# Attention values computed with channels on the partitions and the softmax normalised on GpSimd before the transposes, in a two-block kernel that TensorE fills

## The reference, cut to what matters

```
k_lat, v_lat = mla_kv(z_ckv, z_kr, g_kvnorm[l], w_ukv[l], cos, sin)
k_ctx, v_ctx = mla_kv(zc_ckv, zc_kr, g_kvnorm[l], w_ukv[l], None, None)
q_lat = mla_q(z_cq, g_qnorm[l], w_uq[l], cos, sin)
attn = attend_blocked(q_lat, concatenate([k_ctx, k_lat]), concatenate([v_ctx, v_lat]))
...
s = einsum('bqhd,bkhd->bhqk', q, k) * ATTN_SCALE      # 8 heads, 96 channels
p = softmax(s, axis=-1)
o = einsum('bhqk,bkhd->bqhd', p, v)                   # 64 value channels a head
y = merge_branches(u, conv_module(...), attn @ w_o_mla[l], fourier_mix(...), ...)
if not last:                                          # only in layer 0
    attn_c = attend_dense(q_ctx, k_ctx, v_ctx)        # 256 context queries, 256 keys
```

## Time and profile before

| what | value |
|---|---|
| median of three runs | 2736.62 us (2735.38 to 2741.98) |
| the profiled execution | 2741.98 us |
| span of its instructions | 2740.2 us |
| PE busy | 2623.9 us, 96% of the span |
| DVE, ACT and POOL busy | 62%, 39% and 3% |
| granted TensorE clock, mean | 0.98 |
| attention of layer 0 (first scores to last transposes) | about 1173 to 1294 us |
| attention of layer 1 | about 2355 to 2427 us |

### The profile page before, as it was taken

The page is one execution under the profiler, slowest core; times in us unless marked ns, Lnnn a source line. Parts: engine busy times, 40 slices in busy tenths (PEclk is TensorE's granted clock), DMA queues, the critical chain, the costliest instruction groups (busy, mean ns, idle before and its releaser), DMA issues.

```text
span 2740.2 us, 38792 instructions
## 1 busy us (share of the span) xinstructions
PE 2623.9 (96%) x15874; PEld 2318.9 (85%) x15874; DVE 1711.4 (62%) x2717; ACT 1077.4 (39%) x1652; POOL 69.7 (3%) x64
## 2 busy tenths in 40 slices
PE   7998879799999999999999999999999999998998
PEld 7997669699988888777888888889888888888998
DVE  5766575577777666466654676756555446776664
ACT  5445532445522223334243422323322225555543
POOL 0001013000000000000010000000000000000000
PEclk9999889899999999999999999999999999999999
DMA  6665210267455543211322255543444434244554
GB/s 241 227 216 179 70 45 1 92 230 238 156 177 187 180 160 126 78 42 50 102 89 98 93 187 189 173 169 121 140 136 140 131 99 131 69 140 149 169 190 149
DMA packets 110113, 380.98 MB, mean 139 GB/s; under 512 B 12016, under 2 KB 17392, under 8 KB 109552
## 3 DMA queue, kind: packets, MB, share of 16 engines
q1 hardware_dynamic: 108928, 373.32, 41.0%
q10 hardware_dynamic: 1008, 5.18, 0.5%
HBM read 377.40 MB, written 1.05 MB: 138 GB/s over the span
## 4 chain that ended last, share of the span: by engine, by line
PE 88%; DVE 6%; ACT 4%; issue 2%; DMA 1%; ACTq 0%; SPq 0%; DVEq 0%
PE B L1377 25%; PE B L1378 25%; PE B L1379 25%; ACT w_hi L1677 2%; DVE w_lo L1947 1%; PE B L1616 1%; PE B L1599 1%; PE B L1523 1%; PE B L1392 1%; PE B L1509 1%; PE B L1393 1%; PE B L1394 1%; PE B L1516 1%; PE B L1606 1%; DVE AC L2208 1%
## 5 line engine op out<-in xcount | busy, mean ns | idle before, releaser
L1377 PE MATMUL B<-U,w_hi 128*128 128x256 f32 (+1 forms) x2896 | 964.2, 333 | 9.2 <-DVE w_lo L1947 5.4
L1378 PE MATMUL B<-U,w_hi 128*128 128x256 f32 (+1 forms) x2896 | 955.0, 330 | 0.0
L1379 PE MATMUL B<-U,w_lo 128*128 128x256 f32 (+1 forms) x2896 | 954.8, 330 | 0.0
L1947 DVE TENSOR_TENSOR w_lo<-w_raw,w_hi 128x1024 fp32r<-128x1024 f32 (+4 forms) x587 | 684.3, 1177 | 390.2 <-ACT w_hi L1677 389.4
L1677 ACT ACTIVATE w_hi<-w_raw 128x1024 fp32r<-128x1024 f32 (+4 forms) x587 | 591.0, 1012 | 508.4 <-PE B L1379 484.3
L1377 PEld LDWEIGHTS B<-U,w_hi 128*128 128x128 f32 x2896 | 550.1, 190 | 68.3 <-issue 12.6
L1378 PEld LDWEIGHTS B<-U,w_hi 128*128 128x128 f32 x2896 | 548.6, 189 | 53.4 <-issue 2.0
L1379 PEld LDWEIGHTS B<-U,w_lo 128*128 128x128 f32 x2896 | 548.4, 189 | 51.6
L1377 PE MATMUL B<-HHf,w_hi 128*128 128x256 f32 (+1 forms) x1122 | 364.7, 325 | 1.8 <-DVE w_lo L1947 1.8
L1379 PE MATMUL B<-HHf,w_lo 128*128 128x256 f32 (+1 forms) x1122 | 363.9, 324 | 0.0
L1378 PE MATMUL B<-HLf,w_hi 128*128 128x256 f32 (+1 forms) x1122 | 363.9, 324 | 0.0
(11 more groups left out here) (342 smaller groups left out, 2653.5 us busy)
## 6 DMA issues: line engine op xcount, KB each, us to landing
w_raw<-in_w SPq DMA_DIRECT2D x504, 512.0 KB, 4.2
w_ada<-in_w SPq DMA_DIRECT2D x144, 512.0 KB, 3.4
w_raw<-in_w SPq DMA_DIRECT2D x58, 384.0 KB, 3.2
w_raw<-in_w SPq DMA_DIRECT2D x16, 240.0 KB, 2.5
X<-in_x SPq DMA_DIRECT2D x2, 1024.0 KB, 9.5
w_raw<-in_w SPq DMA_DIRECT2D x8, 256.0 KB, 2.7
BW<-in_bias ACTq DMA_DIRECT2D x1, 1536.0 KB, 10.4
K<-in_consts ACTq DMA_DIRECT2D x2, 640.0 KB, 4.8
```

Of the source, the lines that this page charges most:

```text
L1377: pe.matmul(o, hi, xh, start=i == 0 and s.start, stop=False)
L1378: pe.matmul(o, hi, xl, start=False, stop=False)
L1379: e = pe.matmul(o, lo, xh, start=False, stop=i == last and s.stop)
L1947: dve.tensor_tensor(w_lo[:, plan.slot[u], 0:n], w_raw[:, plan.ring[u], 0:n], w_hi[:, plan.slot[u], 0:n].bitcast(F32), ALU.subtract).then_i ...
```

## The change

For each head and half, the exponentials are normalised before they are transposed: a new step `soft_n`, in a turn of its own between `soft` and `soft_tr`, takes the reciprocal on DVE and multiplies the 128 x 512 or 128 x 256 exponentials by it on GpSimd. The temporary stays held for that turn. `pv` swaps its operands: the 64 value channels of the head are the weights and the 256 queries the columns, and the two heads of a pair write the two halves of the partitions of one PSUM bank, which is held from the first to the last product of the pair. So `soft_o` and `at_tr` go, with the tiles by token, and `at_out` reads the bank of a pair; it is planned when all 8 heads are prepared. The Fourier parts of layer 1 now wait for the first prepared head, and the taps of layer 1 come at 3.5 a turn.

```diff
-TAPS, LATE, WIDTH, WIDTH1 = (4, 6), 4, 8, 6
+TAPS, LATE, WIDTH, WIDTH1 = (4, 7), 4, 8, 6
...
             def soft(h, s):
+                c = h // 2
...
                 yield
+                for i, (sm, t) in enumerate(work):
+                    self.add("soft_n", key=(l, h, s, i), sm=sm, t=t)
+                    SM.done(sm, ("soft_n", (l, h, s, i)))
+                yield
                 yield from PT.room()
                 yield from PS.room(2)
...
-                yield from PS.room()
-                b = PS.get()
-                self.add("pv", key=(l, h, s), b=b, pt=pt)
+                if c not in out:
+                    yield from PS.room()
+                if c not in out:
+                    out[c] = PS.get()
+                    left[c] = 2 * ns
+                self.add("pv", key=(l, h, s), b=out[c], pt=pt)
                 PT.done(pt, ("pv", (l, h, s)))
-                yield
-                self.add("soft_o", key=(l, h, s), b=b, arg=[sm for sm, t in work], need=(old,))
-                PS.done(b, ("soft_o", (l, h, s)))
-                for sm, t in work:
-                    SM.done(sm, ("soft_o", (l, h, s)))
+                left[c] -= 1
+                if not left[c]:
+                    yield
+                    while len(prepared) < 8:
+                        yield
+                    self.add("at_out", key=(l, c), n=n, b=out[c], need=(old, ("mm", ("q", l, 7)), ("pv", (l, h, s))))
+                    PS.done(out[c], ("at_lo", (l, c)))
...
             yield from rounds(tasks, WIDTH)
-            banks = []
-            for c in range(4):
-                yield from PS.room()
-                banks.append(PS.get())
-                self.add("at_tr", key=(l, c), n=n, b=banks[c])
-            for c, b in enumerate(banks):
-                self.add("at_out", key=(l, c), n=n, b=b, need=(old, ("mm", ("q", l, 7))))
-                PS.done(b, ("at_lo", (l, c)))
...
         def fouriers():
             for j in range(4):
-                while not l and len(prepared) < 2 * j + 1:
+                while len(prepared) < (1 if l else 2 * j + 1):
                     yield
...
             elif k == "soft_tr":
-                w.wait_ge(*at("soft_p", s.key))
+                w.wait_ge(*at("soft_n", s.key))
...
-                for i in range(2):
-                    for kc in range(nk // 128):
-                        e = pe.matmul(PS(s.b)[:, 64 * i:64 * i + 64], M2[l]["PT"][:, s.pt.i, kc, 128 * i:128 * i + 128],
-                                      M2[l]["V"][:, k0 // 128 + kc, 64 * h:64 * h + 64], start=kc == 0,
-                                      stop=kc == nk // 128 - 1)
+                for kc in range(nk // 128):
+                    e = pe.matmul(PS(s.b)[p:p + 64, 256 * s_:256 * s_ + 256],
+                                  M2[l]["V"][:, k0 // 128 + kc, 64 * h:64 * h + 64], M2[l]["PT"][:, s.pt.i, kc, :],
+                                  start=kc == 0, stop=kc == nk // 128 - 1)
...
-            elif k == "soft_tr":
+            elif k == "soft_n":
                 w.wait_ge(*at("soft_p", s.key))
                 dve.reciprocal(SM(s.sm, 3, 4), SM(s.sm, 2, 3)).then_inc(*up("soft_r", s.key))
...
+            elif k == "soft_n":
+                nk = 512 if s.key[2] == 0 else 256
+                w.wait_ge(*at("soft_r", s.key))
+                pool.tensor_scalar(TM(s.t, nk), TM(s.t, nk), SM(s.sm, 3, 4), None, ALU.mult).then_inc(*up("soft_n", s.key))
```

More of the change, by code:

```diff
@@ L828, in rope @@
             TM.done(t, ("rope", key))
-        prepared, todo, krt = {}, {}, set()
+        out, left, prepared, todo, krt = {}, {}, {}, {}, set()
         def attention():
@@ L902, in soft @@
                     b = PS.get()
-                    self.add("soft_tr", key=(l, h, s, i), b=b, sm=sm, t=t, pt=pt, need=(("ada", self.last_ada),))
+                    self.add("soft_tr", key=(l, h, s, i), b=b, t=t, pt=pt, need=(("ada", self.last_ada),))
                     TM.done(t, ("soft_tr", (l, h, s, i)))
@@ L1253, in program @@
             shift(n, f"M{l}", st)
-            t2["OT"] = []
-            for half, x in (HI, "H"), (LO, "L"):
-                with ExitStack() as s2:
-                    t2["OT"].append(sb(f"OT{x}{l}", [128, ns, 512], F32, s2))
-                tile = sb(f"AC{x}{l}", [128, 5, n], F32R, st)
+            for half, tile in (HI, sb(f"ACH{l}", [128, 5, n], F32R, st)), (LO, sb(f"ACL{l}", [128, 5, n], F32R, st)):
                 half[f"AT{l}"], half[f"CQ{l}"] = tile[:, 0:4], tile[:, 2:5]
@@ L1337, in src @@
         return PS(s.x[1], s.n)
-    def by_token(l, i):
-        ns = 1 if l else 2
-        return M2[l]["OT"][i // ns][:, i % ns, :]
     def fourier_tables(l):
@@ L1609, in tensor @@
                 l, h, s_ = s.key
-                k0, nk = (0, 512) if s_ == 0 else (256, 256)
+                p, (k0, nk) = 64 * (h % 2), (0, 512) if s_ == 0 else (256, 256)
                 w.wait_ge(*at("soft_pt", (l, h, s_, 1)))
@@ L1613, in tensor @@
                 w.each(s.b.after)
-                for i in range(2):
-                    for kc in range(nk // 128):
-                        e = pe.matmul(PS(s.b)[:, 64 * i:64 * i + 64], M2[l]["PT"][:, s.pt.i, kc, 128 * i:128 * i + 128],
-                                      M2[l]["V"][:, k0 // 128 + kc, 64 * h:64 * h + 64], start=kc == 0,
-                                      stop=kc == nk // 128 - 1)
-                e.then_inc(*up("pv", s.key))
-            elif k == "at_tr":
-                l, c = s.key
-                w.each(s.b.after)
-                for s_ in range(s.n // 256):
-                    w.wait_ge(*at("soft_o", (l, 7, s_)))
-                for i in range(s.n // 128):
-                    e = pe.transpose(hs(PS(s.b), i), by_token(l, i)[:, 128 * c:128 * c + 128], ident)
-                e.then_inc(*up("at_tr", s.key))
+                for kc in range(nk // 128):
+                    e = pe.matmul(PS(s.b)[p:p + 64, 256 * s_:256 * s_ + 256],
+                                  M2[l]["V"][:, k0 // 128 + kc, 64 * h:64 * h + 64], M2[l]["PT"][:, s.pt.i, kc, :],
+                                  start=kc == 0, stop=kc == nk // 128 - 1)
+                e.then_inc(*up("pv", s.key))
             elif k == "four_1":
@@ L1882, in scalar @@
                                PS(s.b, nk).rearrange("p (a b) -> p a b", b=128), ACT.Copy).then_inc(*up("soft_pt", s.key))
-            elif k == "soft_o":
-                l, h, s_ = s.key
-                w.wait_ge(*at("pv", s.key))
-                w.each(s.need)
-                for i, sm in enumerate(s.arg):
-                    w.wait_ge(*at("soft_r", (*s.key, i)))
-                    e = act.activation(by_token(l, 2 * s_ + i)[:, 64 * h:64 * h + 64], PS(s.b)[:, 64 * i:64 * i + 64], ACT.Copy,
-                                       scale=SM(sm, 3, 4))
-                e.then_inc(*up("soft_o", s.key))
             elif k == "at_out":
                 l, c = s.key
-                w.wait_ge(*at("at_tr", (l, 3)))
                 w.each(s.need)
```

## The result

Over four runs of each kernel the median went from 2739.14 us (2735.38 to 2741.98) to 2767.6 us (2759.56 to 2774.58). The ratio is 1.0104, with a 95% interval of 1.0072 to 1.0136: about 28 us slower, 1% and well outside what scatters. The profiled execution took 2764.85 us, and its span is 2763.0 us.

The account below looks back on a forecast made before the run. PE, busy 96% of the span, was taken as the bound, so only its matmul time and idle time count. Gains of 11.0 us and losses of 9.1 us gave -1.9 us from the 2736.62 us median: 2734.7 us, range 2726 to 2744.

Parts of the forecast that it names:

- The multiply's price: New normalising multiply on POOL: 1.0 us for 512 columns, 0.55 for 256, with bounds of 0.6 and 1.74 us.
- The multiply's lateness: Transposes wait for POOL: +1.5 us in layer 0's turns, +2.6 at its last head, +0.5 at layer 1's last two heads.
- The clock: Sign of a wrong forecast: PE loses clock at the new pauses; no term, as the stage before showed none.
- POOL beside DVE: Both attention stages: collisions give DVE 17 us more work, but only the tight places pay, +1.0 us.
- Removed waits: Both attention stages: PE's waits for `soft_o` and before `at_tr` go, 3.0 + 0.7 us and 1.4 us, within -6.2 us together.
- I see no wait: Rival, layer 0's turn 20: held banks could bring 3.7 us of waits back, 2738.4 us; chance included in the sum's 0.60.
- Layer 1's start: PE idles before layer 1's first scores, +2.5 us, and in turns 2 to 4 waits for DVE, +1.0 us.
- Behind layer 1's attention: Fewer taps left after the attention: PE lacks 1.5 instead of 3.4 us there, -1.9 us.
- Values and transposes on PE: Attention on PE: 160 instead of 320 value instructions, -0.3 us, and 24 transposes back fewer, -2.6 us.
- DVE and POOL block each other: Rival: half a collision, 0.53 us, delays transposes at each of 24 head halves, 12.7 us, to 2747.4 us; chance 0.16.

Follow-up runs that it names:

- experiment 2: The changed kernel without the multiply, so the softmax is not normalised; reciprocals and the extra turn stay: 2743.97 us, ratio 0.9987.
- experiment 6: The changed kernel with two unused products of constants on PE before each of 12 waiting transpose groups in layer 0: 2765.99 us, ratio 1.0084.
- experiment 12: The changed kernel without 84 of layer 0's 90 convolution taps, sums incomplete: 2765.59 us in one execution.
- experiment 10: The kernel before, with only layer 1's Fourier parts waiting for the first prepared head; taps as before: 2743.65 us in one execution.
- experiment 9: The changed kernel with multiplies shared by ACT and POOL, layer 1's old gate and taps, `at_out` planned after all values: 2735.92 us, ratio 0.9985 to before.

## Why the prediction was wrong

The forecast was 2734.7 us with a range of 2726 to 2744 us and no measurable change as the likeliest; it came out 28 us slower. Two steps failed. The multiply on POOL was priced at 1.0 us and came at 1.56, so that PE waits 13.8 us for it instead of 5.6. And the lower clock at the new pauses, put at nothing, costs 14.8 us.

The table splits the two stages. PE's pauses are the stage minus PE's busy time. The clock's part is half of the time at the lower level that lies outside these pauses, an estimate: in after, pairs of Fourier matmuls (L1628, L1629) started 0.85 us apart at the lower level (2420.12 to 2421.82 us) and 0.43 us apart at the full clock (1287.97 to 1290.99 us), so work takes twice as long there. What is left should be the same wherever PE's work is the same. Numbers in brackets are those of the experiments.

| stage | us | PE's pauses | clock | left |
|---|---|---|---|---|
| layer 0, before | 390.6 | 6.2 | 0.0 | 384.5 |
| after | 410.0 | 15.5 | 9.2 | 385.3 |
| no multiply (2) | 390.4 | 6.5 | 0.0 | 384.0 |
| constants in the pauses (6) | 405.0 | 7.2 | 3.3 | 394.6 |
| no taps (12) | 397.1 | 10.3 | 1.7 | 385.1 |
| layer 1, before | 244.6 | 14.8 | 1.7 | 228.1 |
| after | 253.4 | 18.6 | 7.3 | 227.5 |
| no multiply (2) | 248.6 | 14.4 | 7.4 | 226.8 |
| before with the gate (10) | 251.7 | 14.1 | 9.1 | 228.6 |

(The 410.0 us are 409.97; the 409.9 above comes from rounded starts.) The last column stays within 2 us in a layer, but for the 10 us of work that experiment 6 adds. Of the 28.1 us, PE's pauses make 9.3 + 3.8 = 13.1 and the clock 9.2 + 5.6 = 14.8.

- **The multiply's price** ("The multiply on POOL ... I take 1.0, and 0.55 for 256 columns"). It is 1.56 and 0.92 us alone. The bounds, 0.6 and 1.74 us, held the truth for the bare operation, and of my two nearest rows I followed the wrong one: a broadcast product with a column of 128 x 512 at 1.04 us says nothing about this form. The 1.235 us from which the lower bound came mixes 512 and 256 columns; the 512-column additions alone took 1.57 us on average, and 24 other two-input operations on 128 x 512 took 1.32, so 1.04 was the quickest of the rows at hand. No term of the sum was worked out at the upper end.
- **The multiply's lateness** ("+1.5", "+2.6", "+0.5 us", with collisions "+1.0"). 5.6 us were forecast and 13.8 us of waits came (9.3 in layer 0, 4.5 in layer 1). The places were right: turns 15 to 16, 19 to 20, and the last head of layer 0, where the waits are 3.5, 2.8 and 2.7 us for 0.9, 0.6 and 2.6 forecast. In turn 16 one of them is 2.66 us, where I had 0.9 in all; its multiply took 3.12 us, 1.56 more than one that meets nothing. The step was right in its mechanism and wrong in size, by the price and by where a collision lands.
- **The clock** ("a PE that loses clock at the new pauses, of which the stage before shows none"). I named it as what would make the forecast wrong and gave it neither a term nor a chance. It is the largest single item, 9.2 us in layer 0 and 5.6 in layer 1. Experiment 6 shows it apart from the waits. With it layer 0 adds up: against experiment 2 the multiply costs 9.0 us of pauses, 9.2 of clock and 1.3 us that stay open, together its 19.5 us. In layer 1 the total isn't the multiply's: without it (experiment 2) the stage has the same 17.1 us at the lower level, and with the gate alone (experiment 10) 20.5 us. Only the places move: of the 17.1 us, 6.8 lie at the waits for POOL in after (from 2416.4 us on), while in experiment 2 10.2 lie at the two pauses of layer 1's start. That the stage before ran at 1.00 was no evidence for after: its pauses stood alone (2.5 us before the first scores, at most 1.2 us for `soft_o`), and the new ones come in groups, 0.46 + 2.66 + 0.42 us within 6 us. Which pauses bring it isn't settled here: experiment 12 has three groups of 2.8, 1.6 and 1.6 us and the lower clock at the first one alone.
- **POOL beside DVE** ("17 us more DVE work"). Wrong side: DVE is busy 3.6 us more in the whole kernel, while POOL's multiplies take 57.8 us for 32 of 512 columns and 17.2 us for 16 of 256, which is 57.8 - 32 x 1.56 + 17.2 - 16 x 0.92 = 10.4 us more than their bare time. One took 5.46 us, though no wait of PE names it. It started at 2388.69 us, 0.12 us after a `split_lo`:

```profile
2388.57 1.23 DVE L1921 TENSOR_TENSOR w_lo<-w_raw,w_hi 128x1024 fp32r<-128x1024 f32 x1 [1.79 <-ACT w_hi L1661]
2389.71 0.41 DVE L2241 TENSOR_TENSOR QK<-B,SSB 96x256 f32<-96x256 f32 x1
2390.05 0.67 DVE L2250 TENSOR_TENSOR QK<-B,SSB 64x512 f32<-64x512 f32 x1
2390.64 1.21 DVE L1921 TENSOR_TENSOR w_lo<-w_raw,w_hi 128x1024 fp32r<-128x1024 f32 x1
2391.78 0.41 DVE L2241 TENSOR_TENSOR QK<-B,SSB 96x256 f32<-96x256 f32 x1
2392.11 0.67 DVE L2250 TENSOR_TENSOR QK<-B,SSB 64x512 f32<-64x512 f32 x1
2392.71 2.03 DVE L2182 SCALAR_TENSOR_TENSOR AC<-VC,PC,AC 128x256 f32<-128x256 f32 x4
```
```profile
L2345 POOL TENSOR_SCALAR TMP<-TMP,SMALL x4: 1562/1564/5464, 2384.1 to 2388.7; 128x512 f32<-128x512 f32 x4
```

  POOL began second and lost to six DVE instructions in a row; the first tap behind them took 0.84 us where the others took 0.47, so in the end DVE waited as well. The Trainium skill ("SBUF — State Buffer", section "Who interferes with whom") has the second one wait for the first; the trace agrees on who waits, but in this one case the wait is not over with that one instruction.
- **Removed waits** ("-6.2 us", and the rival "I see no wait"). The 3.7 us of layer 0 went, and so did the 1.4 and 1.1 us of layer 1. But the values of the last pair waited 2.0 us for the bank of the first (turn 23), which I had looked for in turn 20 only, and small pauses between the pieces took the rest (experiment 2). For layer 0 I had gains of 0.3 + 1.8 + 3.7 = 5.8 us; experiment 2 shows 0.2 us, and experiment 9, with the bank's wait taken out and 1.9 us of waits for POOL left in, 1.6 us.
- **Layer 1's start** ("+2.5 us", "+1.0 us"). Right in place and size for the wait: 3.2 us in after, 2.8 us with the gate alone, and another of 2.0 to 2.4 us for the sums' tile `SSB` that I hadn't seen. Its cost in clock was missed, and by experiment 10 the clock is all that the gate costs: 10.2 us of its 20.5 at the lower level lie at these two pauses.
- **Behind layer 1's attention** ("-1.9 us"). Right in direction and nearly in size: 3.4 us fell to 0.9 in the windows, and all waits there from 10.1 to 6.5. Layer 1's waits were not all for `w_lo`, as the prediction had read them: the 4.4 us without a releaser were among them, and a pause of 4.2 us stands in their place. The table loads went as forecast, five and five to one and one, and were worth nothing that shows.
- **Values and transposes on PE** ("-0.3", "-2.6 us"). Counts and durations right; the swap itself gives nothing, as said.

The rival "DVE and POOL block each other" (chance 0.16, 2747.4 us) ended on the right side and named half of the mechanism: PE's waits of 13.8 us are close to its 12.7, but that is luck: it had half a collision at every head half, and the waits came at 16 transposes, by experiment 12 mostly through the multiply's own length. It too had no clock in it; with the clock's 14.8 us added it would have been at 2762.2 us. What stays open is how the loss that goes away with the taps (12.8 us of layer 0's mixer) divides into collisions and queueing on DVE.

## What to carry to other kernels

An idle engine isn't a free one: what counts for a step on a chain is how soon it is done after its input, and here the idle POOL took 1.56 us for what ACT did in 0.71 and DVE in 0.49. Where PE is busy 96% of the time, price each new pause in a stage of thin work (small transposes, 64- and 96-row products) at its length, and give a chance of its own to the case that a group of them costs up to as much again in lower clock: it did in three groups of after (9.0 us of waits, 9.2 of clock), and in experiment 12 in one of three, where it cost 1.7 us. Take each bound of an unknown price through the tightest turn, not only the middle value.

## What the runs showed of the hardware

- A product of 128 x 512 f32 with a column scalar took 1.56 us on POOL (0.92 us for 256 columns), 0.71 us (0.50) on ACT and 0.49 us (0.35) on DVE; POOL's product of such a tile with a broadcast column took 1.04 us, a third less than with the scalar operand.
- In one case, a POOL multiply that began 0.12 us behind a DVE instruction with two inputs from SBUF took 5.46 us, while DVE ran six of its own.
- At three groups of pauses among transposes (3.5, 2.8 and 2.7 us in all, the longest pause 2.66 us) PE ran 6.8 us at the lower granted clock level each time; with the pauses filled by products of constants, these stretches were gone and the stage became 4.9 us shorter with 10.4 us more work.
- The same pause of 2.5 us before the first scores had 6.8 us at the lower level with it in two of the thirteen executions that have it, and none in eleven; layer 0's same code took 395.1 us with 6.8 us at the lower level and 393.8 us with 3.4.
